# A retrieval layer's tokens split 128 gathered, 384 dense, with both expert tables in one stretch

## The reference

```python
def chunk(xc):                       # xc: 128 tokens
    q = (xc @ w_pq).reshape(P_CHUNK, P_HEADS, 2, P_DK // 2)
    s = jnp.einsum('thpd,hpkd->thpk', q, sub_keys)
    s_top, i_top = lax.top_k(s, P_TOPK)
    cand = s_top[..., 0, :, None] + s_top[..., 1, None, :]
    best, ci = lax.top_k(cand.reshape(P_CHUNK, P_HEADS, P_TOPK * P_TOPK), P_TOPK)
    ...
    expert = e1 * N_KEYS + e2        # 8 heads x 16 experts for each token
    gate = softmax(best)
    act = gelu(einsum('thkd,td->thk', u_tab[expert], xc))
    return einsum('thk,thkd->td', gate * act, v_tab[expert])
```

## Time and profile before

| | us |
|---|---|
| median of 3 runs | 3438.34 |
| lowest, highest | 3436.27, 3440.72 |
| span of the profiled execution | 3437.9 |
| TensorE busy | 3257.9 |
| VectorE busy | 2421.8 |
| ScalarE busy | 1423.2 |

### The profile page before, as it was taken

How to read it: one execution, slowest core, us unless ns; L and a number is a source line. 1 busy time by engine, 2 the same in 40 slices (tenths; PEclk the granted TensorE clock), 3 DMA queues, 4 the chain that set the end, 5 groups by cost and what they waited for, 6 DMA issues and landing times.

```text
span 3437.9 us, 46156 instructions
## 1 busy us (share of the span) xinstructions
PE 3257.9 (95%) x16552; PEld 2770.3 (81%) x16552; DVE 2421.8 (70%) x4512; ACT 1423.2 (41%) x2397; POOL 220.4 (6%) x220
## 2 busy tenths in 40 slices
PE   7998989899999999999999998988999989889998
PEld 5775657699999999999999996756888756578886
DVE  5998995679979946668788776875656566564344
ACT  5336664333334434433433334563423256533232
POOL 0000000000000102212222210000000000000000
PEclk9999999999999999999999999999999999999999
DMA  5242224433447779989999973711566522123232
GB/s 236 97 141 68 87 80 141 171 112 118 147 158 209 213 251 326 327 307 353 354 350 362 352 271 106 153 50 62 170 191 194 174 76 80 43 74 104 95 100 76
DMA packets 156544, 599.80 MB, mean 174 GB/s; under 512 B 16700, under 2 KB 33212, under 8 KB 143198
## 3 DMA queue, kind: packets, MB, share of 16 engines
q1 hardware_dynamic: 98208, 363.13, 30.8%
q0 software_dynamic: 32464, 190.85, 15.5%
q10 hardware_dynamic: 25710, 43.75, 4.4%
HBM read 531.60 MB, written 66.06 MB: 174 GB/s over the span
## 4 chain that ended last, share of the span: by engine, by line
PE 74%; DVE 16%; DVEq 3%; ACT 3%; issue 2%; DMA 1%; PEld 0%; ACTq 0%; PEldq 0%; SPq 0%; POOL 0%; POOLq 0%
PE ps L388 22%; PE ps L390 22%; PE ps L389 22%; DVE w_lo L371 2%; PE ps L2737 1%; DVE nmax L1925 1%; DVE f_sb L1860 1%; DVE A L2051 1%; DVE mod_in L1411 1%; PE ps L448 1%; DVE Pm L1933 1%; DVE B L2054 1%; DMA mod_up<-w_mods 1%; DVEq L1699 1%; PE ps L2291 1%
## 5 line engine op out<-in xcount | busy, mean ns | idle before, releaser
L371 DVE TENSOR_TENSOR w_lo<-raw,w_hi 128x1024 fp32r<-128x1024 f32 x535 | 654.7, 1224 | 481.4 <-ACT w_hi L366 476.3
L388 PE MATMUL ps<-RH,w_hi 128*128 128x512 f32 (+1 forms) x2464 | 941.9, 382 | 50.3 <-DVE RL L493 39.1
L389 PE MATMUL ps<-RL,w_hi 128*128 128x512 f32 (+1 forms) x2464 | 926.6, 376 | 0.0
L390 PE MATMUL ps<-RH,w_lo 128*128 128x512 f32 (+1 forms) x2464 | 926.1, 376 | 0.0
L366 ACT ACTIVATE w_hi<-raw 128x1024 fp32r<-128x1024 f32 x535 | 559.5, 1051 | 442.4 <-PE ps L390 354.6
L388 PEld LDWEIGHTS ps<-RH,w_hi 128*128 128x128 f32 x2464 | 467.6, 190 | 129.8 <-issue 63.4
L390 PEld LDWEIGHTS ps<-RH,w_lo 128*128 128x128 f32 x2464 | 467.0, 190 | 59.9
L389 PEld LDWEIGHTS ps<-RL,w_hi 128*128 128x128 f32 x2464 | 467.9, 190 | 58.6 <-issue 2.2
L388 PE MATMUL ps<-WH,w_hi 128*128 128x416 f32 x1024 | 358.8, 350 | 0.0
L389 PE MATMUL ps<-WL,w_hi 128*128 128x416 f32 x1024 | 358.8, 350 | 0.0
L390 PE MATMUL ps<-WH,w_lo 128*128 128x416 f32 x1024 | 358.7, 350 | 0.0
(11 more groups left out here) (389 smaller groups left out, 4261.4 us busy)
## 6 DMA issues: line engine op xcount, KB each, us to landing
raw<-w_all SPq DMA_DIRECT2D x536, 512.0 KB
mod_in<-w_modr SPq DMA_DIRECT2D x128, 512.0 KB, 4.2
act_scratch<-act_out ACTq DMA_DIRECT2D x128, 208.0 KB
peer_gate_scratch<-Gs POOLq DMA_DIRECT2D x13, 2048.0 KB, 11.9
GL<-peer_gate_scratch POOLq DMA_DIRECT2D x32, 832.0 KB
act_in<-act_scratch POOLq DMA_DIRECT2D x32, 832.0 KB, 10.7
mod_up<-w_mods SPq DMA_DIRECT2D x4, 2048.0 KB, 18.8
Tb<-bias_row_scratch POOLq DMA_DIRECT2D x32, 256.0 KB, 3.0
```

The lines of the kernel that those rows point to most:

```text
L371: nc.vector.tensor_tensor(w_lo[j][:], raw[j][:], w_hi[j][:].bitcast(F32), ALU.subtract).then_inc(lo_done, 1)
L388: nc.tensor.matmul(out_ap, w_hi[slot][:, k, :], rh, start=start and x == 0, stop=False)
L389: nc.tensor.matmul(out_ap, w_hi[slot][:, k, :], rl, start=False, stop=False)
L390: last = nc.tensor.matmul(out_ap, w_lo[slot][:, k, :], rh, start=False, stop=stop and x == n - 1)
```

## The change

Of the 512 tokens, 128 are gathered and 384 are dense (96 and 416 before). The gathered ones are now one block of 128 tokens, one on each partition, with 128 gathers through four `UV` buffers and no fold. The gates run for 12 blocks of 32 tokens.

The last 56 up steps (14 rounds; 13 before) and the 128 down steps form one stretch of 184 steps (`R_F`, 46 rounds) whose order is in the table `ORDER`: up 0, up 1, then up n+2 and down n in turn, then downs alone. The up steps of this stretch leave their activations in SBUF (`up_act`), and weigh takes them from there; only the 18 rounds of earlier chunks go through DRAM. The chunks of the down steps begin with those of this stretch.

A down step now has the activations as the stationary operand and the table as the moving one: for each of two halves of the width and three blocks of 128 tokens, three matmuls of 512 columns, 18 in all, into six banks; two banks are left for the up steps. The sums then have tokens on partitions. At the end ScalarE copies them to `Z`, and TensorE transposes Z and Y, 32 times 128 x 128.

The 16 modulation rows of the down steps move: 8 more lie beside the pointwise and output products, 8 more in the product behind the stretch, where SP waits for the last gathered sum before it loads the first two of them.

The core of the diff:

```diff
-NS, NA, NB = 96, 64, 32
+NS = 128
 ND = T - NS
+NB = ND // P
-GI = (GB + 1) // 2
+GI = GB // 2
+CHUNKS = RING * CHUNK_ROUNDS
+FUSED = RING * LATE
+LAG = 2
+STEPS = FUSED + CHUNKS
+ORDER = [("up", n) for n in range(LAG)]
+for _n in range(CHUNKS):
+    if _n + LAG < FUSED:
+        ORDER.append(("up", _n + LAG))
+    ORDER.append(("down", _n))
+DOT_FUSED = 88
+DOT_AT = {**{4 + k * (2 * FUSED - 4) // DOT_FUSED: k for k in range(DOT_FUSED)},
+          **{2 * FUSED + k * (STEPS - 2 * FUSED - 4) // (NS - DOT_FUSED): DOT_FUSED + k
+             for k in range(NS - DOT_FUSED)}}
+def weigh_step(n):
+    return 2 if n < 2 else 2 * n if n < FUSED else max(2 * FUSED - 1, n + 2 * FUSED - FUSED - 2)
+def low_step(n):
+    if n == 0:
+        return 2
+    if n < FUSED - 1:
+        return 2 * n + 1
+    return weigh_step(n) if n <= FUSED else n + FUSED - 1
         def out_mods(u):
-            return 0 if u < 2 else 2 if u in (8, 9) else 1
+            return 0 if u == 0 else 2 if u >= 7 else 1
 # ScalarE
+            def act_up(n):
+                act.wait_ge(unit_done, RING * R_F + UP_AT[n] + 1)
+                if n >= 2:
+                    act.wait_ge(w_done, n - 1)
+                sc.activation(up_act[n % 2][:], bank(n % 2, ND), ACT.Gelu).then_inc(up_free, 1)
+            for i in range(STEPS):
+                hi_ahead(act, R_F + i // RING, i % RING)
+                if i and ORDER[i - 1][0] == "up":
+                    act_up(ORDER[i - 1][1])
+                for n in WEIGH_AT.get(i, ()):
+                    act_w(n)
+                if i in DOT_AT:
+                    pair_weight(DOT_AT[i])
 # VectorE
+            for i in range(STEPS):
+                lo_ahead(dve, R_F + i // RING, i % RING)
+                if i >= 2 * FUSED:
+                    for n in LOW_AT.get(i, ()):
+                        weigh_low(n)
+                for n in WEIGH_AT.get(i, ()):
+                    weigh(n)
...
+                if i - 1 in DOT_AT:
+                    gathered(DOT_AT[i - 1])
+                if i in DOT_AT:
+                    dot(DOT_AT[i])
 # TensorE
+            def down(i, n):
+                j, last = i % RING, n == CHUNKS - 1
+                pe.wait_ge(wl_done, n + 1)
+                pe.wait_ge(lo_done, RING * R_F + i + 1)
...
+                for h in range(2):
+                    vh, vl = (x[j][:, 4 * h:4 * h + 4, :].rearrange("p a b -> p (a b)") for x in (w_hi, w_lo))
+                    for b in range(NB):
+                        o, tok = bank(2 + h * NB + b), slice(b * P, b * P + P)
+                        mm(o, WH[n % RING][:, tok], vh, start=(n == 0), stop=False)
+                        mm(o, WH[n % RING][:, tok], vl, start=False, stop=False)
+                        ins = mm(o, WL[n % RING][:, tok], vh, start=False, stop=last)
 # VectorE, in the product behind the stretch
             for n in range(8):
                 lo_ahead(dve, R_DSA_IN + n // 4, n % 4)
-                pair_mod(RING * CHUNK_ROUNDS + n)
+                for x in range(2):
...
+                    dve_mod(dve, m % 2, m // 2 + 1, MODX[:, m:m + 1], crow2)
```

More of the change, by code:

```diff
@@ L230, in build @@
         crow1 = at(S + 8, "crow1", [P, D])
[L231 to L235, removed]
+        pair_i = at(S + 66, "pair_i", [P, NS], U32)
+        pair_g = at(S + 66.5, "pair_g", [P, NS])
+        pair_s = at(S + 67, "pair_s", [P, NS])
+        pair_w = at(S + 67.5, "pair_w", [P, NS])
         pair_a = psum_row
-        wf = [at(S + 60 + 1.625 * j, f"wf{j}", [P, ND]) for j in range(2)]
-        def uv_slot(k):
-            return 3 if k >= NB and k % 3 == 2 else k % 3
         KVH = at(S, "KVH", [P, 2, T], F32R)
@@ L706, in _ @@
                         n += 1
-            with sp.Fori(R_PW + 5, R_D + 1) as r:
+            with sp.Fori(R_PW + 5, R_DSA_IN + 1) as r:
                 for j in range(RING):
                     weights(r, j)
+            for u in range(RING, RING + 3):
+                weights(R_DSA_IN + u // RING, u % RING)
+            sp.wait_ge(acc_done, NS)
             for x in range(2):
@@ L712, in _ @@
             n = OUT_MODS + 2
[L713 to L717, removed]
+            for u in range(RING + 3, 4 * RING):
+                weights(R_DSA_IN + u // RING, u % RING)
+                for x in range(2):
+                    if n < MLP_MODS:
+                        modulation(n, n % 2)
+                        n += 1
             with sp.Fori(R_DSA_IN + 4, R_MLP1 + 1) as r:
@@ L2162, in _ @@
+            for k in range(KC):
+                dve.wait_ge(rows_tp, k + 2)
                 v.scalar_tensor_tensor(X[:, k, :], bank(k), MODX[:, 24 + k:25 + k], X[:, k, :],
@@ L2177, in _ @@
                 lo_ahead(dve, R_DSA_IN + n // 4, n % 4)
-                pair_mod(RING * CHUNK_ROUNDS + n)
+                for x in range(2):
+                    m = tl["mod"]
+                    if m == OUT_MODS:
+                        dve.wait_ge(crow_in, 64)
+                    dve_mod(dve, m % 2, m // 2 + 1, MODX[:, m:m + 1], crow2)
+                    tl["mod"] += 1
             dve.drain()
@@ L2722, in _ @@
             for m in range(3):
-                for b in range(TB):
+                for b in range(NB):
                     ins = nc.tensor.transpose(bank(4 + m)[:, b * P:(b + 1) * P],
@@ L2741, in gates @@
                         up_one(i + R_G, i + 11, s // 4)
[L2743 removed]
+            with pe.Fori(0, GI) as i:
                 gates(i, 16)
[L2745 to L2747 removed]
             up(R_G + GI, EARLY - 1)
[L2749 to L2754 removed]
@@ L2769, in _ @@
-            ins.then_inc(e_tp, 1)
+            pe.wait_ge(g_evac, 16 * GI)
+            for k in range(KC):
+                o = bank(4 + k // 4)[:, k % 4 * P:(k % 4 + 1) * P]
+                mm(o, RH[:, k, ND:T].bitcast(F32), ident[:], start=True, stop=False)
+                ins = mm(o, RL[:, k, ND:T].bitcast(F32), ident[:], start=False, stop=True)
+            ins.then_inc(rows_tp, 1)
+            for i, (kind, n) in enumerate(ORDER):
+                if kind == "up":
+                    up_fused(i, n)
+                else:
+                    down(i, n)
@@ L2877 @@
         stream += [wq[i], up[2 * i - 2], up[2 * i - 1]]
-    stream += [up[n] for n in range(6, CHUNK_ROUNDS)]
-    stream += [down[n] for n in range(CHUNK_ROUNDS)]
+    stream += [up[n] for n in range(6, EARLY)]
+    tables = {"up": up.reshape(CHUNKS, P, 8, P), "down": down.reshape(CHUNKS, P, 8, P)}
+    stream.append(np.stack([tables[kind][(n + RING * EARLY) % CHUNKS] for kind, n in ORDER], 0))
     wa = a["a_w_in_2"][0]
```

338 lines of the change are left out of this document (135 added, 203 removed).

## The result

The changed kernel takes 3491.76 us (3486.08 to 3492.39, 4 runs) beside 3439.53 us for the kernel before on the same chip: a ratio of 1.0151, 95% interval 1.0139 to 1.0163. It is slower by 52 us. The forecast was 3469 with a range of 3442 to 3495. The sign and the cause hold; the sum was 22 us short, and more than half of that lies in one term.

The account below looks back on a forecast made before the run. It took TensorE as the bound, with a VectorE-ScalarE ring close under it that the change makes binding; terms 5.5 - 2 - 39.2 + 58 + 0 + 8.3 = +30.6 on 3438.3 gave 3469 us, range 3442 to 3495.

Parts of the forecast that it names:

- The ring: Shared stretch: VectorE and ScalarE wait for each other around each dot, setting the pace; 872 us against 814, +58.
- The decisive step: Shared stretch: ring prices summed over steps; 5.58 us with dot and sum, 529 us for steps 4 to 111, 311 after.
- Rival 1: Shared stretch: TensorE stays the bound, 757 us instead of 872, kernel 3354; chance 0.1.
- Rival 2: Shared stretch ring half as dear, or the cost of the modulation rows hides: 3431 to 3445; chance 0.08.
- Rivals 3 and 4: Shared stretch: transfers bind beside the ring, 3506, chance 0.08; VectorE and GpSimd contend over SBUF, 3502, chance 0.02.
- The columns: TensorE's matmuls: 175 ns at 384 columns, 226 at 512; up step 4.52 to 4.20 us, down step 4.52 to 4.07.
- The rule on weight loads: TensorE down steps: loads overlap matmuls only in different row groups, so fewer loads would save 1.1 us a step; left out.
- The index projection: Behind the shared stretch: 16 modulation rows instead of 8 cost VectorE +11.9; net +8.3 after a covered later wait.
- The cycle of the pairs: Index projection: 6.09 us per buffer cycle for two modulation rows a step, used to size the 16 rows.
- The output product: Before the shared stretch: eight more modulation rows, two buffers binding; 9.2 us of VectorE less 3.7 makes +5.5.
- TensorE's waits that I credited: Output product: the last three X waited for TensorE, 3.7 us together, subtracted from the rows' cost.
- The stage behind the retrieval: Up stage before the shared stretch: TensorE-bound, cheaper and fewer up steps, fewer gate groups and transposes, -39.2.

Follow-up runs that it names:

- the order of ScalarE: Changed kernel with ScalarE making the pair weight one step later, behind the next w_hi: 3376.58 us, ratio to the kernel before 0.9808.
- the order of VectorE: Changed kernel with VectorE doing this step's dot before the weighted sum of the step before: 3395.58 us.
- the spread of the dots: Changed kernel with 60 instead of 88 of its 128 dots in the first 112 steps, 68 in the last 68: 3509.03 us.
- its variant: Kernel before with ScalarE's pair weight made one down step later in its 128 down steps: 3440.91 us, ratio 1.0004.
- the last version: Changed kernel, pair weight later, bias rows held, modulation rows back in their places, three gather buffers, last 8 rows started two steps ahead: 3351.37 us.

## Why the prediction was right, and where its sum was short

**The ring (+58 forecast, +62.4 measured).** The decisive step held in each of its parts. Counted from the w_lo of step 4 (1246.49) and step 112 (1777.00) to that of step 180 (2089.82), the first part takes 530.5 us (529) and the second 312.8 (311), a step with dot and sum 5.58 (5.58). The small operation of 384 columns, estimated at 0.466, is 0.47 from start to start (1305.40 to 1305.87). That the ring and not work or transfers makes it is shown by four runs: the order of ScalarE (-115), the order of VectorE (-96), the spread of the dots (+17), and the gathers gone (0). Rival 1 (3354, TensorE stays the bound) fell, and its condition stood in the text: the gap of 1.54 us has to vanish behind other work. One moved call did that and put the stretch at TensorE's pace: 760.6 us (1225.9 to 1986.5), where that rival had 757. The kernel got to 3376.6 and not to 3354 for these 3.6 us and because the other terms kept their misses, some 18 us together. Rival 2 (ring half as dear) fell with the timeline. Rivals 3 and 4 (3506 and 3502) lay nearer the measured time than my forecast did, and are wrong: the run without gathers and the dots' duration say so. A time near a rival's is no evidence for it.

**The columns.** 384 columns take 173 ns (1228.66 to 1229.18 is three matmuls), interpolated at 175; 512 columns 227 ns. With these the stretch at TensorE's pace was to be 756 us, and the version with the pair weight later took 760.6, with TensorE busy for 759.1 of the 760 us shown. The rule on weight loads that I weighed and left out (the Trainium skill, TensorE: Matmul & The Clock Gate, The mechanism) is contradicted once more: that piece holds 3657 loads, which fill 666 of its 760 us, and matmuls fill 759.1 of them beside the loads.

**The index projection (+11.9 forecast for VectorE, +24.3 measured).** This is the term that was mis-sized. The cycle of the pairs was about right, even a little dear: without the collision the eight rows cost +9.1. What I missed is the next transfer behind them. The bias rows start once ScalarE has passed its norm, which the modulation rows don't hold up: 34.7 us behind the first row (2139.93 to 2174.60), 34.2 in the kernel before (2108.21 to 2142.39). With 16 rows VectorE is still at them then. It stood in the profile before as one DMA of 5 MB; I asked only who waits for mod_in, and not which other queue sends in that window. Held back, it gave the 15.4 us.

**The output product (+5.5 forecast, +9.6 measured).** In the prediction the two buffers bind a step with two rows. The last seven steps in the changed kernel show another bound, which I hadn't read as a ring: w_lo waits 1.65 us "<-ACT w_hi", because ScalarE squares X before it makes the next w_hi. The gap stands in the kernel before too, at 1.65 to 1.78 us. VectorE's timeline:

```profile
650.90 1.23 DVE L408 TENSOR_TENSOR w_lo<-raw,w_hi 128x1024 fp32r<-128x1024 f32 x1 [1.65 <-ACT w_hi L403]
652.04 1.22 DVE L1450 SCALAR_TENSOR_TENSOR mod_in<-mod_in,crow 128x1024 f32<-128x1024 f32 x1
...
654.05 1.23 DVE L1450 SCALAR_TENSOR_TENSOR mod_in<-mod_in,crow 128x1024 f32<-128x1024 f32 x1 [0.78 <-DMA mod_in<-w_modr]
655.20 0.75 DVE L2065 SCALAR_TENSOR_TENSOR X<-ps,MODX,X 128x512 f32<-128x512 f32 x1
657.59 1.23 DVE L408 TENSOR_TENSOR w_lo<-raw,w_hi 128x1024 fp32r<-128x1024 f32 x1 [1.65 <-ACT w_hi L403]
```

The ring alone makes 5.83 us a step (645.07 to 650.90); where a buffer's transfer lands late on top of it, 6.69 (650.90 to 657.59). Each row lies in full on that ring, the waits for mod_in with it (2.6 us in all, 0.2 before), and TensorE's waits that I credited give back 3.7: 9.2 + 2.4 - 3.7 = 7.9 of the 9.6. The other 1.7 us don't belong to the rows. They arise in the first 33 us, in code that the change leaves alone: the last 16 matmuls on `mod_up`, from 28.7 us on, take 3.62 us at a granted clock of 0.55, where the kernel before has 1.92 us at 1.00, and the first w_lo starts at 32.97 instead of 31.25. The profiles of the changed kernel and of its eight variants show the later start (first w_lo at 32.4 to 33.1), those of the kernel before and its variant don't (31.3). Why is open. These 1.7 us are a part of the 22 by which the sum was short, and no term of the prediction stood for them.

**The rest.** The stage behind the retrieval gave 36.0 of 39.2; TensorE has 226 us of work in 234 there. The retrieval gave 0.9 of 2. Behind the stretch 3.4 us came off that I had put at nothing: X starts 0.8 us after the last matmul of the stretch (2105.38 against 2104.6) instead of 3.7 us. The last part came within 0.4 us.

## What to carry to other kernels

Ask of a stage not only which engine is busiest, but whether two engines wait for each other once a step, and add that loop up in time: its length is the sum of the operations on it and of the gaps, and it becomes the bound where that passes the busiest engine's step, with no engine full. Then look whether a result is made earlier in an engine's order than its user needs it; moving it behind the operation that others wait for cost nothing in either kernel here. And when work grows longer by some microseconds, look at every queue for the next large transfer that it will now meet.

## What the runs showed of the hardware

A transfer that lies on another queue delays one started behind it. Two modulation rows of 0.5 MB, started 0.8 us and more after the 5 MB of bias rows, were used 16 and 20 us after 2175.37, against a median of 4.3 us from issue to landing for these rows; with the large transfer held back VectorE waited 0.24 and 0.68 us for them. The stretch of the collision in the changed kernel:

```profile
2174.60:2192.00 17.40, 1.27 (x8) 0.57 (x4) 3.32 (x6) 0.66 (x2) 0.00 (x0) 0.63 0.96 171
```

The DMA engines are full (0.96) at only 171 GB/s, where the shared stretch of the last version moved 363 GB/s at 0.93; the bias rows go to memory and need 54.7 us to land. The Trainium skill (DMA: Bandwidth & Descriptors, Queues, rings and completion order) says that a DMA engine takes turns between its queues, a packet from each. The trace agrees in that the small rows land long before the large transfer; they share with it and don't stand behind it.

TensorE's granted clock followed its gaps in the shared stretch, and cost nothing visible there. In the changed kernel it was 0.97 from 1240 to 1750 (0.95 in the 100 us from 1340, with TensorE busy for 90), so mostly the 2.4 GHz level with some time at 1.2; with the ring opened it was 1.00 in the same piece. The steps kept the 5.58 us that the ring gives, so a slower TensorE only filled its own gaps. At the start of the kernel it did cost: 16 matmuls that VectorE waits for took 3.62 us at 0.55, mostly the 1.2 GHz level, and 1.92 at 1.00 in the kernel before. TensorE had been idle for much the same time ahead of them, 2.99 us and 2.81, so the idle time just before them doesn't tell the two apart.
